# A float32 two-model kernel on one core: raw rows transposed ahead of the first expert layer, ring slots freed in pairs, heads and sums in another order

## The reference

```python
        h = h + (gate_a * y_a + gate_b * y_b) @ w_o[l]
        h = h + peer_ffn(rmsnorm(h, g_ffn[l]), w_q[l], sub_keys[l], expert_u[l], expert_v[l])

def rmsnorm(x, g):
    y = xf * lax.rsqrt(jnp.mean(xf * xf, axis=-1, keepdims=True) + RMS_EPS)
    return (y * g.astype(jnp.float32)).astype(x.dtype)

# peer_ffn, 8 heads, 16 of 128 x 128 experts per head and token
    q = (xb @ w_q).reshape(TOK_BLOCK, PEER_HEADS, 2, PEER_DHALF)
    s = jnp.einsum('thcd,hcnd->thcn', q, sub_keys)
    top_s, top_i = lax.top_k(s, K)                 # K = 16 of 128, for each half
    cand = top_s[:, :, 0, :, None] + top_s[:, :, 1, None, :]
    best_s, best_c = lax.top_k(cand.reshape(TOK_BLOCK, PEER_HEADS, K * K), K)
    ...
    gate = jax.nn.softmax(best_s, axis=-1)
    u = expert_u[e]
    act = jax.nn.gelu(jnp.einsum('td,ted->te', xb, u), approximate=False)
    return jnp.einsum('te,ted->td', gate * act, expert_v[e])
```

## Time and profile before

| what | us |
|---|---|
| median of 3 runs | 2518.23 (2517.28 to 2520.91) |
| the profiled execution | 2512.19 |
| its span | 2510.4 |
| PE busy | 2232.6 (89%) |
| DVE busy | 1659.9 (66%) |
| ACT busy | 913.5 (36%) |
| POOL busy | 865.9 (34%) |

### The profile page before, as it was taken

How to read it: one execution, slowest core, us unless ns; L and a number is a source line. 1 busy time by engine, 2 the same in 40 slices (tenths; PEclk the granted TensorE clock), 3 DMA queues, 4 the chain that set the end, 5 groups by cost and what they waited for, 6 DMA issues and landing times.

```text
span 2510.4 us, 30004 instructions
## 1 busy us (share of the span) xinstructions
PE 2232.6 (89%) x9846; PEld 1277.0 (51%) x9846; DVE 1659.9 (66%) x3971; ACT 913.5 (36%) x2668; POOL 865.9 (34%) x796
## 2 busy tenths in 40 slices
PE   9989989989988889989989988889899989977776
PEld 7877745544454445545545554435555535523222
DVE  3864566666665677666677666667667767777664
ACT  2232233333343434343443334434335533433232
POOL 0012044344333343333334343234333444344442
PEclk9999999999999999999999999999999999999999
DMA  5421589999999999999999999999999999999996
GB/s 195 134 69 36 196 346 421 421 421 421 421 420 421 416 386 421 420 421 421 419 406 421 421 416 421 394 422 416 421 419 406 407 420 421 421 421 420 418 418 279
DMA packets 151656, 942.30 MB, mean 375 GB/s; under 512 B 16864, under 2 KB 19136, under 8 KB 53072
## 3 DMA queue, kind: packets, MB, share of 16 engines
q0 software_dynamic: 110592, 805.36, 77.5%
q1 hardware_dynamic: 40912, 135.05, 14.0%
HBM read 939.29 MB, written 1.05 MB: 375 GB/s over the span
## 4 chain that ended last, share of the span: by engine, by line
PE 41%; DMA 41%; DVE 9%; ACT 5%; issue 3%; POOL 0%; DVEq 0%; ACTq 0%; POOLq 0%
DMA arena<-in_uv,idx 40%; PE bank L1909 24%; PE bank L371 5%; DVE arena L1937 5%; PE bank L1546 2%; ACT arena L1975 1%; PE bank L1558 1%; PE bank L844 1%; PE bank L865 1%; DMA weights<-in_sb_v 1%; PE bank L602 1%; DVE arena L1215 1%; ACT arena L1963 1%; PE bank L831 1%; ACT arena L1969 1%
## 5 line engine op out<-in xcount | busy, mean ns | idle before, releaser
L1909 PE MATMUL bank<-arena 128*128 128x512 f32 x3072 | 1438.4, 613 | 239.9 <-ACT arena L1975 233.0
L1994 POOL DMA_INDIRECT arena<-in_uv,idx x768 | 838.2, 1091 | 1423.1 <-PE bank L1909 1299.0
L1909 PEld LDWEIGHTS bank<-arena 128*128 128x128 f32 x3072 | 569.4, 194 | 946.7 <-issue 594.0
L1937 DVE CUSTOM_DVE_ANT_0 arena<-arena,h 128x1024 f32<-128x1024 f32 x512 | 627.4, 1225 | 399.7 <-DMA arena<-in_uv,idx 395.1
L1963 ACT ACTIVATE arena<-arena 128x2 f32<-128x2 f32 x384 | 78.1, 203 | 1194.1 <-DVE arena L1937 1193.9
L1937 DVE CUSTOM_DVE_ANT_0 arena<-arena 128x1024 f32<-128x1024 f32 x256 | 313.9, 1226 | 215.1 <-DMA arena<-in_uv,idx 213.8
L371 PEld LDWEIGHTS bank<-xT,weights 128*128 128x128 f32 x1808 | 250.6, 191 | 51.9 <-issue 34.9
L371 PE MATMUL bank<-xT,weights 128*128 128x128 f32 (+2 forms) x1808 | 269.3, 304 | 0.0
L1975 ACT ACTIVATE arena<-const,arena 128x128 f32<-128x128 f32 x768 | 260.5, 386 | 0.0
L1969 ACT ACTIVATE arena<-arena 128x1 f32<-128x1 f32 x768 | 184.8, 288 | 12.6
L1963 ACT ACT_TABLE_LOAD x73 | 93.7, 1283 | 1.3
(11 more groups left out here) (333 smaller groups left out, 1850.9 us busy)
## 6 DMA issues: line engine op xcount, KB each, us to landing
weights<-in_w_q SPq DMA_DIRECT2D x42, 512.0 KB, 8.6
weights<-in_w_in SPq DMA_DIRECT2D x38, 512.0 KB, 3.5
weights<-in_a_fm SPq DMA_DIRECT2D x28, 512.0 KB, 9.2
arena<-in_uv,idx POOLq DMA_INDIRECT x768, 13.9
weights<-in_a_out SPq DMA_DIRECT2D x16, 512.0 KB, 8.2
weights<-in_b_fm SPq DMA_DIRECT2D x16, 512.0 KB, 7.8
weights<-in_b_out SPq DMA_DIRECT2D x16, 512.0 KB, 9.8
arena<-in_w_q SPq DMA_DIRECT2D x14, 512.0 KB, 13.2
```

The costliest lines, as they stand in the source:

```text
L1909: ins = nc.tensor.matmul(acc[:, :], diag[:, e % DIAGS, :], ring[:, e % RING, at:at + 512], start=first, stop=last)
L1937: V.tensor_tensor_reduce(out=u, in0=u, in1=x, scale=1.0, scalar=0.0, op0=ALU.mult, op1=ALU.add, accum_out=dots[:, unit % 2, kx:kx + 1]).th ...
L1994: nc.gpsimd.indirect_dma_start(out=ring[:, s, :], out_offset=None, in_=io[f"uv{unit // PH // NT}"], in_offset=bass.IndirectOffsetOnAxis(ap ...
```

## The change

Five things change together.

1. TensorE transposes h itself (`fm_tensor(pe, 0, i, h)`), as soon as the residual is added. VectorE evicts the transposes and multiplies them by g_ffn (`raw_in`, new; the column of g_ffn lies doubled in `cols`). The root goes in as the scale of the score copy. The normalized rows xn are still made, for the dot products.
2. Both halves of tile 1's projection stand behind head 0's scores, and both gate products inside unit 0's steps, behind the 9th and the 19th.
3. Head 1 comes ahead of tile 1's output product on TensorE. ScalarE does head 1 before the Exp of unit 0, and head 2 behind its first pair.
4. `w_o` moves to slots 3 to 6 and `mix` to slot 7. TensorE signals after each second block of the product, and gathers 3, 4, 5 wait for one such signal each, gather 6 for the end. `last_residual_in` moves behind the third dot product. The w_o blocks are loaded in the order 0, 1, 2, 3, 5, 4, 6, 7.
5. Tile 1's transposes, its norm, and the queries of heads 3 to 7 move some slots later (`first_slot` by one).

The diff, without the table of column names and their host code:

```diff
@@ build
-        mix = A.view(3 * 2 * D, KC, TOK)
-        w_o = A.view(4 * 2 * D, KC, D)
+        mix = A.view(7 * 2 * D, KC, TOK)
+        w_o = A.view(3 * 2 * D, KC, D)
@@ mixed_out
+            if i and kc % 2 and kc < KC - 1:
+                ins.then_inc(sem("w_o_pair_used"), 1)
@@ one_tensor
             rwkv_transposed(pe, 1)
-            rwkv_out(pe, 1, 0)
@@ one_vector
             for half in range(2):
                 v.wait_ge(*banks.emptied(("w_o", 0, half)))
+            raw_in(v, 0)
             variance(v, 0, 0)
             first_apply(v, 0)
@@ new
+        def raw_in(v, i):
+            at = COLS["g_ffn"][0]
+            for half in range(2):
+                v.wait_ge(*banks.full(("xT", 0, i, half)))
+                out = banks.bank(("xT", 0, i, half))
+                ins = nc.vector.tensor_tensor(xT[:, 4 * half:4 * half + 4, cols_of(i)],
+                                              out[:, :].rearrange("p (a b) -> p a b", a=4),
+                                              bc(cols[:, at + 8 * half:at + 8 * half + 8], (2, 4), (0, P)), ALU.mult)
+                ins.then_inc(banks.emptied_sem(("xT", 0, i, half)), 1)
@@ first_slot
-            return PH * group - 23 + step
+            return PH * group - 22 + step
@@ score_out
+            scale = 1.0
+            if job[1] == 0:
+                act.wait_ge(sem(f"norm_var_{i}"), 2)
+                scale = small[:, 2 + i:3 + i]
@@ first_tensor
-            fm_tensor(pe, 0, 0, xn)
+            fm_tensor(pe, 0, 0, h)
             fm_wait(pe, 0, 0)
             early_head(0, 0)
+            rwkv_out(pe, 1, 0)
             rwkv_out(pe, 1, 1)
+            early_head(1, 0)
             for kc in range(KC):
                 mixed_out(pe, 1, kc, (acc_lo, acc_hi), None)
-            early_head(1, 0)
             early_head(2, 0)
             yield 1
-            fm_tensor(pe, 0, 1, xn)
+            fm_tensor(pe, 0, 1, h)
+            yield 2
             fm_wait(pe, 0, 1)
@@ first_scalar
-            fm_scalar(act, 0, 0)
             early_head(0, 0)
+            early_head(1, 0)
             softmax_exp(act, 0)
-            early_head(1, 0)
+            yield 0
+            early_head(2, 0)
+            yield 2
             norm_squares(act, 0, 1)
-            early_head(2, 0)
-            yield 0
+            yield 4
             norm_root(act, 0, 1)
-            yield 1
-            fm_scalar(act, 0, 1)
@@ stream_vector
-            mix_in(v, 1, 0)
             for n_op in range(TOPK_OPS):
                 next(ops)
-                if n_op == 11:
+                if n_op == 8:
+                    mix_in(v, 1, 0)
+                if n_op == 18:
                     mix_in(v, 1, 1)
-            last_residual_in(v)
...
+                    if e == GROUP:
+                        last_residual_in(v)
@@ stream_gpsimd
-                    if e == 3:
+                    if 3 <= e < 6:
+                        pool.wait_ge(sem("w_o_pair_used"), e - 2)
+                    if e == 6:
                         pool.wait_ge(sem("w_o_last"), 2)
@@ beside_vector
-            yield 0
+            yield 3
+            raw_in(v, 1)
+            yield 4
             variance(v, 0, 1)
+            yield 5
             first_apply(v, 1)
```

More of the change, by code:

```diff
@@ L80 @@
                   ("conv_b", 4), ("conv_ln_g", 4), ("conv_ln_b", 4), ("conv_w", CT * TAPS),
-                  ("b_gate", 3), ("head_g", 6)):
+                  ("b_gate", 3), ("head_g", 6), ("g_ffn", 16)):
     COLS[_name] = (_n, _w)
@@ L1488, in normed @@
         def normed(engine, m, i):
-            if m == 0:
-                engine.wait_ge(sem(f"normed_{i}"), 1)
+            if m == 0 and i == 0:
+                for half in range(2):
+                    engine.wait_ge(*banks.emptied(("w_o", 0, half)))
+            elif m == 0:
+                engine.wait_ge(sem("w_o_last_added"), 2)
             else:
@@ L1524, in fm_scalar @@
                 out = banks.bank(("xT", m, i, half))
-                to = xw[:, 4 * half:4 * half + 4, :] if m else xT[:, 4 * half:4 * half + 4, cols_of(i)]
-                ins = nc.scalar.activation(to,
+                ins = nc.scalar.activation(xw[:, 4 * half:4 * half + 4, :],
                                            out[:, :].rearrange("p (a b) -> p a b", a=4), ACT.Copy)
                 ins.then_inc(banks.emptied_sem(("xT", m, i, half)), 1)
+        def raw_in(v, i):
+            at = COLS["g_ffn"][0]
+            for half in range(2):
+                v.wait_ge(*banks.full(("xT", 0, i, half)))
[4 more added lines that the diff above has]
+                ins.then_inc(banks.emptied_sem(("xT", 0, i, half)), 1)
         def plain(act, job, to, n=P, scale=1.0):
@@ L1691, in score_out @@
             at = (score_area(w) * PH * 2 + lo) * NKEYS
-            nc.scalar.activation(scores[:, at:at + (hi - lo) * NKEYS], out[:, 0:(hi - lo) * P], ACT.Copy).then_inc(
-                banks.emptied_sem(job), 1)
+            scale = 1.0
+            if job[1] == 0:
+                act.wait_ge(sem(f"norm_var_{i}"), 2)
+                scale = small[:, 2 + i:3 + i]
+            nc.scalar.activation(scores[:, at:at + (hi - lo) * NKEYS], out[:, 0:(hi - lo) * P], ACT.Copy,
+                                 scale=scale).then_inc(banks.emptied_sem(job), 1)
         def early_scores(pe, group, i, queries):
@@ L2838, in _ @@
                 sp.wait_ge(*banks.full(("O", 1, par)))
-            for kc in range(KC):
-                if kc == 2:
+            for kc in (0, 1, 2, 3, 5, 4, 6, 7):
+                if kc == 4:
                     for par in range(2):
@@ L2903, in lay_out @@
                                 i["conv_w"][0].reshape(TAPS, CT, P).transpose(2, 0, 1).reshape(P, -1),
-                                column(i["a_b_gate_2"][0]), column(i["a_head_g_2"][0].reshape(-1))], 1)
+                                column(i["a_b_gate_2"][0]), column(i["a_head_g_2"][0].reshape(-1)),
+                                np.repeat(column(i["g_ffn"][0]), 2, 1)], 1)
     a["w_conv_out"] = half_fm_blocks(i["w_conv_out"][0])
```

## The result

| what | before | after |
|---|---|---|
| median | 2517.76 us (4 runs, 2517.05 to 2520.91) | 2486.28 us (4 runs, 2481.15 to 2489.57) |
| ratio | | 0.9867, 95% interval 0.9852 to 0.9882 |
| span of the profiled execution | 2510.4 us | 2479.3 us |

The kernel is 31.5 us faster. The prediction said 8.7 us and 2509.5; its range, 2506 to 2515, misses the time by 20 us.

A forecast was written before the change was run, and what follows sets the result against it. The prediction took the kernel after the ramp to be bound by gathers at the DMA's 422 GB/s. Earlier start 2.0, pauses 7.6 and -0.9 given back sum to 8.7 us less than 2518.2: 2509.5 us, range 2506 to 2515.

The forecast's parts named there:

- a gather costs 2.49 us: In the stream from 362 us on, each 1.049 MB gather was taken to flow at 422 GB/s.
- first gather earlier: Ahead of the stream: queries 3.5 us earlier, less 1.44 for a second projection pair inside the top-16, gain 2.0 us.
- pauses up to 380 us: After the first gather, 318 to 362 us: DMA idle time vanishes, 7.6 us, less 0.9 us given back to slower issues.
- The rest at nothing: Queries of heads 3 to 7 later, w_o's loading order and 16 more columns in a small table: priced at nothing.
- What was given back: Gathers 8 to 11, issued during VectorE's dot products, issue more slowly: -0.9 us, bounds 0 and -4.3.
- the 0.9 us lost in 318 to 338: DMA time lost between 318 and 338 us before the change, counted as wholly recovered.
- the 7.6: DMA idle time of 318 to 362 us, claimed to go whole: 0.9 + 3.5 + 3.3 us.
- The pairs: Second output sum: freeing slots by pairs keeps the DMA from running dry from 322.9 to 327.6, 4.7 us.
- Heads 3 to 7 a slot late: In the stream, scores asked for 1.6 us before they are there, five times; priced at nothing.
- The case that priced them at 25 us: Rival, chance 0.04: the late heads' wait costs a whole slot, 2 x 2.49 us, each time with the ring dry; 2534.5 us.
- All four cases: Forecast 2509.5 us (0.72), thin queue 2512.9 (0.13), only the head start 2516.2 (0.11), heads a slot late 2534.5 (0.04).

The follow-up runs named there:

- e1: The kernel before with only 64 unused bytes per partition behind the table of columns, moving the ring to byte 74240: 2497.74 us against 2517.3, ratio 0.9922.
- e2: The changed kernel with g_ffn's columns in their own tensor behind the arena, so the ring stays at its old place: 2508.21 us against 2517.3, ratio 0.9964.
- e10: The changed kernel with tile 0's normalized rows transposed again, evicted by ScalarE, and its scores copied without a scale: 2489.24 us, ratio 0.9881.
- e5: The changed kernel measured again without any edit: 2485.2 us against 2515.13 for the kernel before, ratio 0.9883.
- e7: The changed kernel with 192 unused bytes behind the columns and 320 ahead of the arena, every loaded tensor on a multiple of 512: 2489.62 us, ratio 0.9893.
- e12: The changed kernel with every loaded tensor on a multiple of 512, the same kernel as e7 measured once more: 2483.57 us (6 runs), ratio 0.9871.
- e8: The changed kernel with gathers 3 to 5 waiting for the end of tile 1's output product, not one pair of blocks each: 2491.5 us, ratio 0.9898.
- e11: The kernel before with 128 unused bytes per partition, arena at byte 74304, 64 above a multiple of 256: ratio 1.0022 to the kernel before.

## Why the prediction was wrong

**The step that failed is the first one: a gather costs 2.49 us, with the sum made of when gathers start and where the DMA pauses.** I took the 422 GB/s behind the ramp for a property of the chip and let it stand for both kernels. It was one of this layout. The change moved the ring by 64 bytes, the rate rose by 1.1%, from 421 to 425 and 426 GB/s, and a gather cost 2.46 to 2.47 us, which e1 measures as 19.6 us. Term by term:

| term | forecast | measured |
|---|---|---|
| first gather earlier (from tile 1's transposes to it: 23.97 before, 21.76 after) | 2.0 | 2.2 |
| pauses up to 380 us (lost against the rate: 9.9 before, 3.1 after) | 7.6 - 0.9 = 6.7 | 6.8 |
| schedule in all (e2) | 8.7 | 9.1 |
| place of the ring (e1) | 0, not in the sum | 19.6 |

The first term holds in every trace: 23.96 to 23.99 us in the six with the old schedule, 21.74 to 21.76 in the seven with the new one other than e10. Up to 380 us the other traces with all of the new schedule (e2, e5, e7, e12) lose 2.6 to 2.8 us.

**"The rest at nothing" held the cause.** The prediction names the 16 more columns in a small table and calls them nothing, since their load is long done. The load is nothing. But the table pushes every tensor behind it, the whole arena among them, 64 bytes further. In the list of edits it was the only one that touched all 768 gathers.

**What was given back** was put at 0.9 us, and here luck helped the sum. Gather 6 was issued beside a dot product in 1.75 us and the ninth in 1.16, but the ninth came with the last of the eight still flowing, and the three windows from 338 to 380 us are at 426 to 428 GB/s. So nothing was given back there. Against that, the 0.9 us lost in 318 to 338 did not go, as the 7.6 had it: 0.8 are still lost in the changed kernel's window (409 GB/s), in e5 about 0.2. In the profiled execution the two errors cancel. The price of an issue was also read from too few rows. Of the issues from 340 to 2300 us in the changed kernel, those that lie half a microsecond or more beside a dot product (324 counted) have a median of 0.94 us and a mean of 1.30, those beside none (199) a mean of 0.96; only some reach 1.9. Gather 0's issue took 1.11 us before and after.

**The pairs** are worth about what was said. The DMA would be dry for 4.7 us without them; e8 shows 5.3.

**Heads 3 to 7 a slot late**: waits of 1.6 us, five times, as worked out, and hidden as worked out, since the DMA is at its full share in the same stretch (426 GB/s). The case that priced them at 25 us did not come.

**The range.** It took in only unknowns of the schedule. All four cases shared one rate of the DMA, so their differences could not bound its error. A rate that multiplies 768 gathers of 2.49 us, about three quarters of the time, deserved a bound of its own. One percent of that is 19 us, more than twice the whole forecast gain.

## What to carry to other kernels

In a kernel that is bound by DMA like this one, with rows of 8 KB landing in SBUF, let the buffers that receive them start on a multiple of 256 bytes in the partition, and look at their addresses after each edit of any tensor in front of them. 64 unused bytes were worth twice as much here as a reordering of four engines. And when a small edit of a table or a constant stands in a diff, ask what it moves, not only what it costs.

## What the runs showed that I had not expected

- Where a ring slot starts decides the rate of the gathers: 426 GB/s from 2000 to 2400 us on a multiple of 256 bytes, 420 to 421 at 64, 128 or 192 above one.
- The mixer in front of the stream doesn't start alike in every execution. In e7's profiled execution TensorE's first projection took 5.70 us at 21.86,

```profile
21.86 5.70 PE L493 MATMUL bank<-xT,weights 128*128 128x272 f32 x16
```

and 3.83 us at 17.65 in the changed kernel (e12, the same kernel as e7: 3.83 us at 17.88). The granted clock is 0.50 from 14 to 22 us there, 1.00 in the changed kernel, and the first gather is 8 us or more later (e8 and e11 had the same). The other traces with one schedule start their stream some 5 us apart, without that (312.98 in the changed kernel, 315.10 in e5, 318.18 in e2). It spreads single executions of one kernel, and makes differences of 3 us hard to tell from whole times. The distance from the first gather to the end is steadier (2166.3, 2166.7 and 2166.5 us in the changed kernel, e5 and e12), but no sure measure either: e2's execution shows next to nothing of its gain in it, and e8 takes 2176.5 us, 10 more than e5, where 5.3 are seen at the gap.
